# Head pairs in the softmax, norm factors moved to the evictions, and residual additions four tiles wide

## The chip, the cores and the metric

One program on one core of a Trainium2 chip (trn2). The metric is the time on the device in microseconds (us). The engines are named as the profile names them: PE (TensorE, matmuls), DVE (VectorE), ACT (ScalarE), POOL (GpSimd), SP (SyncE, which here only issues DMAs).

## What is computed

Two transformer blocks on one sequence of 256 tokens, width 2048, in float32, the second block with a memory of 256 tokens. Of the reference only what the change touches:

```python
def first_block(x, ...):
    ...
    y = merged @ w_o
    x = x + rmsnorm(y, g_post_mix)
    h = rmsnorm(x, g_pre_mlp)
    f = jnp.square(jax.nn.relu(h @ w_up)) @ w_down
    return x + rmsnorm(f, g_post_mlp)

def second_block(x, mem, ...):
    p = rmsnorm_2(x, mix_norm_w) @ w_in
    h = x + concatenate([deltanet_group(p[:DN_COLS]), rwkv7_group(p[DN_COLS:])]) @ w_out
    h = h + memory_cross_attention(rmsnorm_2(h, xa_norm_w), rmsnorm_2(mem, mem_norm_w), wq, wk, wv, wo)
    h = h + squared_relu_mlp(rmsnorm_2(h, ffn_norm_w), w1, w2)
    return rmsnorm_2(h, final_norm_w)

def rmsnorm(x, g):
    return x * lax.rsqrt(jnp.mean(x * x, axis=-1, keepdims=True) + EPS) * g

def memory_cross_attention(hn, mn, wq, wk, wv, wo):
    scores = einsum('bshd,bmhd->bhsm', hn @ wq, mn @ wk) * 128 ** -0.5
    return einsum('bhsm,bmhd->bshd', softmax(scores), mn @ wv) @ wo
```

## The kernel before

**Layout.** Activations lie transposed: a tile is 128 features (partitions) by 256 tokens, so the width 2048 is 16 tiles. `resid` holds the residual stream, `work` 64 tiles of scratch, `xa` and `xb` the inputs of the matmuls. A norm sums squares over features, that is over tiles and partitions.

**A matrix product** (class `Gemm`) is split in three. A float32 value is kept as `hi` (rounded) and `lo` (the rest), both for the weights and for the activations. SP loads a *slab*, 512 by 256 weights, into one of four ring slots (`raw`); ACT writes `hi` (L307), DVE `lo = raw - hi` (L343, the "split"); PE does 8 matmuls with `hi` on 512 columns (L428: activation `hi` and `lo`) and 8 with `lo` on 256 (L435). Two tiles of output are a *block*: 4 slabs where the depth is 2048. PE's results lie in two PSUM banks in turn (`pg`); ACT copies half of a block out (`half`, L317), DVE adds the other (the *eviction*, L348 to L397). The eviction has kinds: `store` (one DVE instruction), `add` (two), `normed` (two: sum, then times `rs`), `relu2` (four without a norm, L380 to L396; five with one).

**Order.** Each engine's queue is written out by hand, stage after stage: glu, qkv, gates, sb_out, conv_out, w_o, mem_k, mem_v, then `ff1` (four times w_up, w_down), dn, gab, rw, w_out, xa_q, xa_o, and `ff2` (four times w1, w2). A queue is strictly in order; a slab's `hi` waits until PE has used the slab four before it. What lies beside a product is hooked in: `each` is a generator that is advanced once behind every slab, `after` a function called behind every block. In every queue the next product's first slabs (`follows`) are split before the last eviction.

**Norms.** Squares come from ACT (L496, two buffers `sq`). Their sum is made by POOL into `sq_sum` (L583, for the norms in `POOLED`) and one matmul with ones (L592), or for norms 2 and 4 by 16 matmuls (`norm_pe`, L649). ACT makes `rs = exp(-0.5 * ln(...))` (L522, L523), each with a table load.

- *w_o to up0.* `norm_add_steps` (L682, L687) multiplies each tile of y by its gain and `rs` and adds it to `resid`, two tiles per slab of mem_k and mem_v, with squares and PE's sums beside. Behind mem_v `norm_split_dve` (L661, L666) and `norm_split_act` (L597) make `xa` with `rs` in it, tile by tile. POOL forms the memory's sum of squares between (L542, L547).
- *Last w_down to dn.* The same functions, with nothing beside them.
- *dn.* Behind each block DVE does a short convolution (L1082, L1084), ACT its Sigmoid (L1098), and from block 8 on squares and roots for the l2 norms (L1131, L1126, L1127, PE L1117). In rw the chunk work of the delta rule is hooked in behind slabs, and before it the gates (PE L1188).
- *Cross-attention* (`xat_pe`, `xat_act`, `xat_dve`): behind xa_q, all four heads at once: scores (L1891), transposes of the values (L1895), maximum, subtraction, Exp (L1917), sum, reciprocal, product, transposes (L1902), copy, outputs (L1909), `hi` and `lo` for xa_o.
- *xa_q and w1* already take their input without the norm factor: `xa` is `resid` times the gain (L600, L632), the root comes beside the product's first slabs (`total_later`, `root_later`), and the eviction multiplies by `rs`.

Of the kernel before, what the change touches and what calls it, by code (L numbers as in the profile page):

```python
# [132 lines left out]
def build_program(nc, a, out):  # L133
# [3 lines left out]
    with ctx:  # L137
# [396 lines left out]
        POOLED = (0, 1, 3, 5, 6, 7)  # L534
# [134 lines left out]
        def norm_add_dve(dve, n, added, tile0, gain):  # L669
            rest_of(norm_add_steps(dve, n, added, tile0, gain))  # L670

        def norm_add_steps(dve, n, added, tile0, gain, tmp=half):

            norm_rs_dve(dve, n)
            for k in range(DT + 1):
                if k and k % 2 == 0:
                    yield
                if k < DT:
                    if k >= 2:
                        dve.wait_ge(norm_res, DT * added + k - 1)  # L680
                    seq["dve"] += 1
                    nc.vector.scalar_tensor_tensor(out=tmp[:, k % 2], in0=work[:, tile0 + k, PAD:COLS],  # L682
                                                   scalar=gain(k), in1=rs[:, :], op0=ALU.mult,
                                                   op1=ALU.mult).then_inc(dve_seq, 1)
                if k:
                    dve.wait_ge(dve_seq, seq["dve"] - (1 if k < DT else 0))
                    nc.vector.tensor_tensor(resid[:, k - 1], resid[:, k - 1], tmp[:, (k - 1) % 2],  # L687
                                            ALU.add).then_inc(norm_res, 1)


# [1577 lines left out]
```

## Time and profile before

| | |
|---|---|
| median of 3 runs | 3017.79 us (3017.3 to 3023.87) |
| profiled execution | 3016.97 us, span 3014.9 us |
| PE busy | 2843.5 us, 94% of the span |
| DVE, ACT, POOL busy | 1993.4 (66%), 1439.7 (48%), 172.8 us (6%) |
| TensorE's granted clock, mean | 0.972 |
| read from HBM | 481 MB, 161 GB/s over the span |

Busy is the time in which an engine has an instruction at work. The granted clock is the share of TensorE's full clock. A wait is put down to the instruction that ended it.

### The profile page before, as it was taken

Reading aid. Unit: us, or ns where it says so; the run is one execution under the profiler, and the core shown is the slowest. Engines: PE = TensorE matmul, PEld = TensorE weight load, DVE = VectorE, ACT = ScalarE, POOL = GpSimd, SP = SyncE. Lnnn points to the kernel's source line nnn. Section 1 sums busy time; section 2 is a strip of 40 time slices with the busy share of each in tenths; the row PEclk is TensorE's granted clock in tenths of the full one; section 3 lists DMA queues with packets and bytes.
Section 4 is the critical chain, followed back from the end, with each engine's and each line's share of the span. In section 5 each row is a group of like instructions: output and inputs, shape, how many; then the busy total and the mean of one; then the engine's idle time right before and its main releaser. Section 6 shows DMA issues by size and latency. Waiting matters only on the chain.

```text
span 3014.9 us, 51495 instructions
## 1 busy us (share of the span) xinstructions
PE 2843.5 (94%) x19508; PEld 2485.8 (82%) x19508; DVE 1993.4 (66%) x2502; ACT 1439.7 (48%) x1857; POOL 172.8 (6%) x193
## 2 busy tenths in 40 slices
PE   7999999998999999999799899589979999999997
PEld 6888887877888888888688788478768888888886
DVE  6798886767646566565786666644767656566665
ACT  4545656564444444444547533634545444444443
POOL 3000000240000000001000000031112000000001
PEclk9999999999999999999899999789999999999998
DMA  5665554755666666666355444101535665656664
GB/s 186 188 195 168 175 171 137 223 169 157 190 188 189 188 187 189 188 188 188 105 181 161 128 125 128 34 4 44 163 103 181 191 189 187 189 187 190 188 188 131
DMA packets 481999, 486.66 MB, mean 161 GB/s; under 512 B 14913, under 2 KB 479809, under 8 KB 481841
## 3 DMA queue, kind: packets, MB, share of 16 engines
q1 hardware_dynamic: 480288, 478.55, 51.3%
q0 software_dynamic: 1552, 5.93, 0.6%
q8 instruction: 108, 1.77, 0.2%
q14 instruction: 51, 0.41, 0.0%
HBM read 481.28 MB, written 3.15 MB: 161 GB/s over the span
## 4 chain that ended last, share of the span: by engine, by line
PE 43%; DVE 5%; ACT 2%; issue 1%; DVEq 0%; POOLq 0%; POOL 0%; ACTq 0%
PE pg L428 24%; PE pg L435 12%; PE p L977 1%; DVE lo L343 1%; PE p L994 1%; PE p L1356 1%; PE pg L1597 0%; ACT hi L307 0%; DVE rw_xx L1048 0%; DVE half L682 0%; DVE xa L632 0%; PE p L972 0%; DVE dnc L1084 0%; PE pg L1618 0%; PE p L997 0%
## 5 line engine op out<-in xcount | busy, mean ns | idle before, releaser
L343 DVE TENSOR_TENSOR lo<-raw,hi 128x1024 fp32r<-128x1024 f32 x900 | 1091.7, 1230 | 722.5 <-ACT hi L307 718.1
L307 ACT ACTIVATE hi<-raw 128x1024 fp32r<-128x1024 f32 x900 | 942.4, 1058 | 1104.4 <-PE pg L435 1083.8
L428 PE MATMUL pg<-xa,hi 128*128 128x512 f32 x4224 | 1074.5, 396 | 16.4 <-DVE xa L666 14.2
L428 PEld LDWEIGHTS pg<-xa,hi 128*128 128x128 f32 x4224 | 764.0, 190 | 161.7 <-issue 21.8
L428 PE MATMUL pg<-xb,hi 128*128 128x512 f32 x3008 | 769.4, 398 | 31.6 <-DVE xb L487 15.5
L428 PEld LDWEIGHTS pg<-xb,hi 128*128 128x128 f32 x3008 | 549.3, 191 | 135.6 <-issue 16.6
L435 PEld LDWEIGHTS pg<-xa,lo 128*128 128x128 f32 x4224 | 577.8, 191 | 42.6 <-DVE lo L343 0.7
L435 PE MATMUL pg<-xa,lo 128*128 128x256 f32 x4224 | 590.0, 283 | 0.3 <-DVE lo L343 0.3
L435 PEld LDWEIGHTS pg<-xb,lo 128*128 128x128 f32 x3008 | 412.5, 191 | 34.5 <-DVE lo L343 4.9
L435 PE MATMUL pg<-xb,lo 128*128 128x256 f32 x3008 | 421.7, 283 | 2.8 <-DVE lo L343 2.7
L317 ACT ACTIVATE half<-pg 128x512 f32<-128x512 f32 x220 | 128.3, 583 | 91.0 <-PE pg L435 89.1
L700 DVE SCALAR_TENSOR_TENSOR work<-u,vec,work 128x256 f32<-128x256 f32 x240 | 116.2, 484 | 7.6
L360 DVE TENSOR_TENSOR half<-pg,half 128x512 f32<-128x512 f32 x96 | 65.8, 685 | 40.6 <-ACT half L317 40.1
L587 POOL COPY sq_sum<-sq 128x256 f32<-128x256 f32 x5 | 3.9, 777 | 1436.1 <-ACT sq L496 1436.1
L583 POOL TENSOR_TENSOR sq_sum<-sq_sum,sq 128x256 f32<-128x256 f32 x75 | 74.6, 995 | 178.7 <-ACT sq L496 173.9
L356 DVE TENSOR_TENSOR work<-pg,half 128x512 f32<-128x512 f32 (+1 forms) x74 | 50.5, 683 | 1.4 <-ACT half L317 1.4
L1048 DVE TENSOR_TENSOR rw_xx<-rw_xx,p 128x512 f32<-128x512 f32 x40 | 25.9, 684 | 37.3 <-PE p L997 37.1
L396 DVE TENSOR_TENSOR xb<-sq,xb 128x512 f32 (+1 forms) x64 | 44.3, 692 | 7.8 <-DVE xb L393 0.8
L362 DVE TENSOR_TENSOR resid<-resid,half 128x512 f32<-128x512 f32 (+1 forms) x56 | 41.5, 741 | 5.0 <-DVE half L360 3.9
L380 DVE TENSOR_TENSOR sq<-pg,half 128x512 f32<-128x512 f32 x64 | 43.7, 683 | 0.0
L1010 ACT ACTIVATE rw_tt<-p 128x256 f32<-128x256 f32 (+1 forms) x48 | 18.4, 383 | 48.2 <-PE p L977 39.3
L496 ACT ACTIVATE sq<-resid 128x256 f32<-128x256 f32 x80 | 31.9, 409 | 19.0 <-DVE resid L687 15.7
(401 smaller groups left out, 1709.1 us busy)
## 6 DMA issues: line engine op xcount, KB each, us to landing
raw<-w_in SPq DMA_DIRECT2D x264, 512.0 KB, 4.7
raw<-ffn_w SPq DMA_DIRECT2D x256, 512.0 KB, 4.4
raw<-w_up SPq DMA_DIRECT2D x128, 512.0 KB, 4.0
raw<-w_down SPq DMA_DIRECT2D x128, 512.0 KB, 4.3
raw<-w_o SPq DMA_DIRECT2D x32, 512.0 KB, 4.7
raw<-w_out SPq DMA_DIRECT2D x32, 512.0 KB, 3.5
raw<-w_sb_out SPq DMA_DIRECT2D x16, 512.0 KB, 4.6
raw<-w_conv_out SPq DMA_DIRECT2D x16, 512.0 KB, 4.5
```

The costliest lines, as they stand in the source:

```text
L307: nc.scalar.activation(hi[:, slot], raw[:, slot], ACT.Copy).then_inc(hi_ready, 1)
L317: nc.scalar.activation(half[:, :, :], pg[:, par, :, T:2 * T], ACT.Copy).then_inc(half_out, 1)
L343: nc.vector.tensor_tensor(lo[:, slot], raw[:, slot], hi[:, slot].bitcast(F32), ALU.subtract).then_inc(lo_ready, 1)
L356: nc.vector.tensor_tensor(place, psum, half[:, :, :], ALU.add).then_inc(evacuated, 1)
L360: nc.vector.tensor_tensor(half[:, :, :], psum, half[:, :, :], ALU.add).then_inc(summed, 1)
L362: nc.vector.tensor_tensor(place, place, half[:, :, :], ALU.add if g.kind == "add" else ALU.mult).then_inc(evacuated, 1)
L380: nc.vector.tensor_tensor(sq[:, :, :], psum, half[:, :, :], ALU.add).then_inc(summed, 1)
L396: nc.vector.tensor_tensor(rest, sq[:, :, :], place.bitcast(F32), ALU.subtract).then_inc(evacuated, 1)
L428: nc.tensor.matmul(pg[:, par, t, :], lhsT=hi[:, slot, k, c:c + P], rhs=g.x[:, kk, :], start=(j == 0 and k == 0), stop=False)
L435: ins = nc.tensor.matmul(pg[:, par, t, 0:T], lhsT=lo[:, slot, k, c:c + P], rhs=g.x[:, kk, 0:T], start=False, stop=(j == g.groups - 1 and k ...
L583: ins = nc.gpsimd.tensor_tensor(sq_sum[:, :], sq_sum[:, :], sq[:, k % 2], ALU.add)
L700: ins = nc.vector.scalar_tensor_tensor(out=acc, in0=x, scalar=v1("w_dw", 8 * j + c), in1=acc, op0=ALU.mult, op1=ALU.add)
```

## The change

Five parts:

1. `w_up` gets `norm=2`; `dn`, `gab` and `rw` change from `store` to `normed` with `norm=4`. Their input `xa` is then `resid` times the gain alone; `rs` is multiplied in at each eviction.
2. Behind w_o and behind the last w_down, ACT squares a tile of y and multiplies it by its gain in place (`y_act`), beside the product. DVE then multiplies four tiles by `rs` in one instruction (`y_scale_dve`); the addition to `resid`, four tiles wide, is DVE's for quarters 0 and 2 and GpSimd's for 1 and 3.
3. Squares of the new `resid` are taken four tiles wide into the place of y. They are added up ("folded") four tiles wide: behind w_o by GpSimd, behind w_down by DVE beside dn's first block. PE's 16 sums become one matmul. All norms are now in `POOLED`.
4. POOL does the memory's squares two tiles per step and is done with them earlier; the totals stand one slab later.
5. The cross-attention works by pairs of heads; the first pair's scores and softmax and the value transposes lie beside the second block of xa_q. The maximum goes into Exp's bias, which drops the subtraction.

```diff
-            up = Gemm(plan, f"up{p}", a["w_up"], D, p * D, D, xa, "relu2", (xb, 0, 0))
+            up = Gemm(plan, f"up{p}", a["w_up"], D, p * D, D, xa, "relu2", (xb, 0, 0), norm=2)
...
-        g_dn = Gemm(plan, "dn", w2in, D, 0, 4096, xa, "store", (work, DQ, PAD))
+        g_dn = Gemm(plan, "dn", w2in, D, 0, 4096, xa, "normed", (work, DQ, PAD), norm=4)
...
-        POOLED = (0, 1, 3, 5, 6, 7)
+        POOLED = tuple(range(8))
...
+        y4 = lambda q: work[:, YS + 4 * q:YS + 4 * q + 4, PAD:COLS]
+        resid4 = lambda q: resid[:, 4 * q:4 * q + 4]
+        def y_act(act, e, n, k, weight):
+            square_tile(act, n, k, work, PAD, YS)
+            y = work[:, YS + k, PAD:COLS]
+            nc.scalar.activation(y, y, ACT.Copy, scale=weight(k)).then_inc(y_weighted, 1)
...
+        def y_scale_dve(dve, e, q, n):
+            norm_rs_dve(dve, n)
+            dve.wait_ge(y_weighted, DT * e + 4 * q + 4)
+            nc.vector.tensor_tensor(y4(q), y4(q), rs[:, None, :].to_broadcast([P, 4, T]), ALU.mult).then_inc(y_ready, 1)
+        def y_add_dve(dve, e, q):
+            dve.wait_ge(y_ready, 4 * e + q + 1)
+            nc.vector.tensor_tensor(resid4(q), resid4(q), y4(q), ALU.add).then_inc(added_dve, 1)
+        def y_add_pool(pool, e, q):
+            pool.wait_ge(y_ready, 4 * e + q + 1)
+            nc.gpsimd.tensor_tensor(resid4(q), resid4(q), y4(q), ALU.add).then_inc(added_pool, 1)
...
+        def next_act(act, e, n, q, weight):
+            wait_added(act, e, q)
+            for k in range(4 * q, 4 * q + 4):
+                nc.scalar.activation(xa[:, k, 0:T], resid[:, k], ACT.Copy, scale=weight(k)).then_inc(norm_hi, 1)
+            nc.scalar.activation(y4(q), resid4(q), ACT.Square).then_inc(norm_sq, 4)
+        def next_dve(dve, m, q, weight):
+            for k in range(4 * q, 4 * q + 4):
+                gained_dve(dve, m, weight, k)
+        def fold(dve, e, n):
+            add = (nc.vector if e else nc.gpsimd).tensor_tensor
+            dve.wait_ge(norm_sum, POOLED.index(n))
+            steps = [(y4(0), y4(0), y4(q)) for q in range(1, 4)]
+            steps += [(work[:, YS:YS + 2, PAD:COLS], work[:, YS:YS + 2, PAD:COLS], work[:, YS + 2:YS + 4, PAD:COLS])]
...
+            add(sq_sum[:, :], work[:, YS, PAD:COLS], work[:, YS + 1, PAD:COLS], ALU.add).then_inc(norm_used, DT)
...
+            for q in (1, 3):
+                y_add_pool(pool, 0, q)
+            fold(pool, 0, 2)
...
-            norm_add_dve(dve, 3, 1, 16, lambda k: v1("g_post_mlp", k))
-            norm_rs_dve(dve, 4)
-            norm_split_dve(dve, 2, xa, resid, 0, 0, lambda k: v2("mix_norm_w_2", k), 96)
+            y_scale_dve(dve, 1, 0, 3)
+            y_add_dve(dve, 1, 0)
+            y_scale_dve(dve, 1, 1, 3)
+            next_dve(dve, 2, 0, mix_w)
+            y_scale_dve(dve, 1, 2, 3)
+            y_add_dve(dve, 1, 2)
+            y_scale_dve(dve, 1, 3, 3)
+            for q in range(1, 4):
+                next_dve(dve, 2, q, mix_w)
...
-            norm_total(pe, 3)
-            norm_pe(pe, 4)
-            gemm_pe(pe, g_dn, lambda m: l2_pe(pe, m), x_tiles=96)
+            norm_total(pe, 3)
+            def mix_total():
+                yield from skip(4)
+                norm_total(pe, 4)
+                yield
+            gemm_pe(pe, g_dn, lambda m: l2_pe(pe, m), x_tiles=96, each=step_of(mix_total()))
...
         def xat_pe(pe):
+            turn_pe(pe, 0)
             XA_.act.wait(pe, "v")
+            scores_pe(pe, 1)
+            outputs_pe(pe, 0)
+            turn_pe(pe, 1)
+            outputs_pe(pe, 1)
```

On DVE, the last block of mem_v. Before, its splits (L343) alternate with two tiles of the residual step, the multiplication (L682) and the addition (L687):

```order
L343 TENSOR_TENSOR lo<-raw,hi 128x1024 [waits hi_ready]
L682 SCALAR_TENSOR_TENSOR work<-work,vec,rs 128x256 [waits norm_res]
L687 TENSOR_TENSOR resid<-resid,work 128x256 [waits dve_seq]
L682 SCALAR_TENSOR_TENSOR work<-work,vec,rs 128x256 [waits norm_res]
L687 TENSOR_TENSOR resid<-resid,work 128x256 [waits dve_seq]
```

After, with the changed file's line numbers (L344 split, L682 `y_scale`, L618 `next_dve`, L367 and L370 eviction):

```order
L344 TENSOR_TENSOR lo<-raw,hi 128x1024 [waits hi_ready]
L682 TENSOR_TENSOR work<-work,rs 128x4x256 [waits y_weighted,norm_rs]
L344 TENSOR_TENSOR lo<-raw,hi 128x1024 [waits hi_ready]
L618 SCALAR_TENSOR_TENSOR xa<-resid,vec,xa 128x256 [waits norm_hi] x4
L344 TENSOR_TENSOR lo<-raw,hi 128x1024 [waits hi_ready]
L618 SCALAR_TENSOR_TENSOR xa<-resid,vec,xa 128x256 [waits norm_hi] x4
L344 TENSOR_TENSOR lo<-raw,hi 128x1024 [waits hi_ready]
L618 SCALAR_TENSOR_TENSOR xa<-resid,vec,xa 128x256 [waits norm_hi] x4
L367 TENSOR_TENSOR half<-pg,half 128x512 [waits half_out]
L370 TENSOR_TENSOR work<-half,work 128x2x256 [waits mem_rs,summed]
```

The fourth `y_scale` stands behind the split of slab 12, and the making of `xa` has moved from behind mem_v in between its splits 13, 14 and 15.

On PE, between the product xa_q and xa_o. Before (L1891 scores, L1895 values, L1902 transposes, L1909 outputs):

```order
L1891 MATMUL p<-work 128x256 [waits evacuated,kv_in]
L1891 MATMUL p<-work 128x256 x7
L1895 MATMUL pg<-cst,work 128x128 x8
L1902 MATMUL p<-cst,xs 128x128 [waits xat_dve]
L1902 MATMUL p<-cst,xs 128x128 x15
L1909 MATMUL p<-xp,xv 128x256 [waits xat_dve,xat_act]
L1909 MATMUL p<-xp,xv 128x256 x7
```

After, from the second slab of xa_q's last block (L1932 scores, L1938 values, L1948 transposes, L1956 outputs; L425 and L432 are the slabs):

```order
L1932 MATMUL p<-work 128x256 [waits evacuated,kv_in]
L1932 MATMUL p<-work 128x256 x3
...
L1938 MATMUL p<-cst,work 128x128 x8
...
L1948 MATMUL p<-cst,xs 128x128 [waits xat_dve]
L1948 MATMUL p<-cst,xs 128x128 x7
L1932 MATMUL p<-work 128x256 [waits evacuated,xat_act]
L1932 MATMUL p<-work 128x256 x3
L1956 MATMUL pg<-xp,xv 128x256 [waits xat_dve]
L1956 MATMUL pg<-xp,xv 128x256 x3
```

Four scores and the value transposes have moved in front of the last two slabs of xa_q; transposes and outputs come in two halves.

## Rows read from the trace of the kernel before

**Rows 1.** The page, busy us (share of the span) x instructions.

```profile
PE 2843.5 (94%) x19508; PEld 2485.8 (82%) x19508; DVE 1993.4 (66%) x2502; ACT 1439.7 (48%) x1857; POOL 172.8 (6%) x193
```

**Rows 2.** Busy time of each engine in seven stretches; columns in its head.

```profile
core 0: us, PE busy (x) PEld busy (x) DVE busy (x) ACT busy (x) POOL busy (x), PEclk, DMA share, GB/s
648.90:711.30 62.40, 56.54 (x294) 47.98 (x292) 36.50 (x55) 35.98 (x54) 7.91 (x10) 0.95 0.44 137
711.30:719.30 8.00, 0.18 (x2) 0.00 (x0) 6.34 (x13) 3.58 (x7) 0.87 (x1) 0.81 0.75 236
1435.90:1467.00 31.10, 13.72 (x39) 7.08 (x38) 19.53 (x46) 18.85 (x37) 3.60 (x4) 0.73 0.14 40
1677.80:1685.50 7.70, 0.19 (x2) 0.00 (x0) 2.36 (x6) 7.58 (x11) 0.00 (x0) 0.78 0.31 93
1685.50:1900.00 214.50, 209.09 (x2169) 184.92 (x2169) 135.53 (x200) 86.29 (x129) 0.00 (x0) 0.99 0.42 119
2218.40:2250.10 31.70, 13.74 (x58) 11.31 (x56) 14.54 (x10) 5.50 (x5) 0.00 (x0) 0.78 0.00 1
2290.00:2990.00 700.00, 700.00 (x4009) 615.93 (x4008) 442.52 (x472) 301.31 (x328) 10.49 (x12) 1.00 0.60 186
```

**Rows 3.** Waits of PE: in total, times, longest us.

```profile
PE pg L428 <- DVE xa L666: 14.2, 2, 7.9
```

**Rows 4.** Timeline of PE, w_o to up0: start, us, instructions, [idle before].

```profile
648.93 2.00 PE L428 MATMUL pg<-xb,hi 128*128 128x512 f32 x8
651.73 2.00 PE L428 MATMUL pg<-xb,hi 128*128 128x512 f32 x8
...
660.83 3.97 PE L428 MATMUL pg<-xb,hi 128*128 128x512 f32 x8
...
719.36 3.75 PE L428 MATMUL pg<-xa,hi 128*128 128x512 f32 x8 [7.88 <-DVE xa L666]
...
723.93 2.00 PE L428 MATMUL pg<-xa,hi 128*128 128x512 f32 x8
```

**Rows 5.** Three lines of code: duration ns min/median/max, first and last start.

```profile
L632 DVE SCALAR_TENSOR_TENSOR xa<-resid,vec,xa x32: 471/955/968, 2169.6 to 2287.0; 128x256 fp32r<-128x256 f32 x32
L583 POOL TENSOR_TENSOR sq_sum<-sq_sum,sq x75: 722/990/1722, 586.6 to 3001.0; 128x256 f32<-128x256 f32 x75
L1828 POOL TENSOR_TENSOR rw_br<-rw_br,cst x4: 2352/2360/2367, 1975.9 to 2067.7; 128x1024 f32<-128x1024 f32 x4
```

**Rows 6.** Timeline of DVE, the eviction of `xa_q`.

```profile
2209.69 0.68 DVE L373 TENSOR_TENSOR half<-pg,half 128x512 f32<-128x512 f32 x1
2210.41 0.69 DVE L376 TENSOR_TENSOR work<-half,rs 128x512 f32<-128x512 f32 x1
```

**Rows 7.** Timelines in dn: two of DVE, then four of ACT.

```profile
1544.47 3.50 DVE L343 TENSOR_TENSOR lo<-raw,hi 128x1024 fp32r<-128x1024 f32 x3 [1.65 <-ACT hi L307]
...
1549.43 0.68 DVE L356 TENSOR_TENSOR work<-pg,half 128x512 f32<-128x512 f32 x1
...
1542.86 0.63 ACT L1098 ACTIVATE work<-dnc 128x512 f32<-128x512 f32 x1 [5.29 <-DVE dnc L1084]
...
1554.03 0.63 ACT L1098 ACTIVATE work<-dnc 128x512 f32<-128x512 f32 x1 [5.28 <-DVE dnc L1084]
...
1607.17 0.61 ACT L1131 ACTIVATE sq<-work 128x512 f32<-128x512 f32 x1
...
1622.30 0.62 ACT L1131 ACTIVATE sq<-work 128x512 f32<-128x512 f32 x1
```

**Rows 8.** Timelines behind the last w_down: three of ACT, then PE.

```profile
1444.15 1.28 ACT L523 ACT_TABLE_LOAD   x1
1445.44 0.42 ACT L523 ACTIVATE rs<-rs 128x256 f32<-128x256 f32 x1
...
1486.51 0.63 ACT L1098 ACTIVATE work<-dnc 128x512 f32<-128x512 f32 x1 [3.51 <-DVE dnc L1084]
...
1467.01 3.72 PE L428 MATMUL pg<-xa,hi 128*128 128x512 f32 x8 [6.29 <-DVE xa L666]
```

More of the change, by code:

```diff
@@ L667, in norm_split_dve @@
                                             x[:, k - 1, 0:T].bitcast(F32), ALU.subtract).then_inc(x_ready, 1)
-        def norm_add_dve(dve, n, added, tile0, gain):
-            rest_of(norm_add_steps(dve, n, added, tile0, gain))
-        def norm_add_steps(dve, n, added, tile0, gain, tmp=half):
-            norm_rs_dve(dve, n)
[L675 to L688, printed above, removed]
+        YS = 16
@@ new lines, in turn_pe, with outputs_pe @@
+                        ins = nc.tensor.transpose(all4[:, 4 * q + 2 * kh + h % 2, m * P:(m + 1) * P],
+                                                  xs[:, 2 * h + m, kh * P:(kh + 1) * P], const("ident"))
+            XA_.pe.done(ins, f"p{q}")
+        def outputs_pe(pe, q):
+            XA_.dve.wait(pe, f"p{q}")
+            for h in heads(q):
+                for kh in range(2):
+                    ins = nc.tensor.matmul(xo_psum(q)[:, h % 2], lhsT=xv[:, h, kh], rhs=xp[:, 4 * q + 2 * kh + h % 2],
+                                           start=(kh == 0), stop=(kh == 1))
+            XA_.pe.done(ins, f"o{q}")
@@ new lines, in xat_beside_pe, with xat_pe, xat_exp @@
+        def xat_beside_pe(pe, n):
+            yield
+            yield
+            norm_total(pe, n)
+            yield
+            yield
+            yield
+            pe.wait_ge(kv_in, 16)
+            scores_pe(pe, 0)
+            yield
+            values_pe(pe)
+            yield
+        def xat_pe(pe):
+            turn_pe(pe, 0)
+            XA_.act.wait(pe, "v")
+            scores_pe(pe, 1)
+            outputs_pe(pe, 0)
+            turn_pe(pe, 1)
+            outputs_pe(pe, 1)
+        def xat_exp(act, q):
+            XA_.dve.wait(act, f"nmax{q}")
+            for i in range(4 * q, 4 * q + 4):
+                ins = nc.scalar.activation(xs[:, i], all4[:, i], ACT.Exp, scale=XA_D ** -0.5, bias=xm[:, i:i + 1])
+            XA_.act.done(ins, f"exp{q}")
@@ L2121, in post_mix @@
             def post_mix():
+                yield from skip(3)
+                y_scale_dve(dve, 0, 0, 1)
                 yield
+                y_add_dve(dve, 0, 0)
                 yield
[L2124 removed]
+                y_scale_dve(dve, 0, 1, 1)
+                yield
+                y_scale_dve(dve, 0, 2, 1)
+                yield
+                y_add_dve(dve, 0, 2)
+                yield
+                y_scale_dve(dve, 0, 3, 1)
+                yield
+                for q in range(4):
+                    next_dve(dve, 1, q, pre_mlp_w)
+                    yield
             norms = post_mix()
```

236 lines of the change are left out of this document (145 added, 91 removed).

## Prediction

> **What bounds the kernel now.** First the page's busy shares: TensorE (PE) is busy 94% of the span [rows 1]. So an edit pays only where PE waits or works for nothing. Then a table of stretches [rows 2] shows where that is. In the feed-forward of the second block PE is busy 700.0 of 700.0 us, although every eviction of `w1` there already has the form that the change gives to `w_up`. PE loses time in four places: while `mem_k` and `mem_v` run (62.4 us) and just behind them (8.0), between the last `w_down` and `dn` (31.1, of which 17.4 idle), before the gates of `rw` (7.7), and in the cross-attention (31.7, of which 18.0 idle). The waits of PE [rows 3] name one of the releasers: the `xa` tiles that DVE finishes late.
>
> What is ideal is read from PE's timeline [rows 4]: a slab of weights (8 matmuls `hi`, 8 `lo`) takes 651.73 - 648.93 = 2.79 us. Behind a pause the `hi` half alone takes 3.7 to 4.0 instead of 2.0: the 8 us pause has a granted clock of 0.81 in [rows 2], the first matmuls run at 1.2 GHz, and that costs about 1.8 us each time.
>
> **Part 1, w_o to up0.** Today slab 1 of `up0` starts at 723.93 [rows 4], 75.0 us after the first slab of `mem_k`. The change removes the pause before the totals, the 16 sums of squares by matmul between the slabs, and the wait for `xa` at 719.36. Left are 16 slabs (44.7) and two totals (about 0.9): slab 0 of `up0` could start at 694.5, slab 1 at 697.3, 26.6 us earlier.
>
> But the port stands against it. DVE and GpSimd disturb each other: the same DVE instruction of 256 columns takes 0.47 us or, in its median, 0.955; the GpSimd adds beside it take 0.72 at best and 0.99 in the median [rows 5]. The two take turns, and DVE loses 0.48, which is the 0.72 of the add less 0.24. GpSimd's additions of 1024 columns take 2.36 [rows 5]; by the same subtraction each costs a DVE instruction with two SBUF inputs 2.1 us. The lower bound is 0.48, the upper 2.36; I take 2.1, since the small add shows nearly its whole length. The Trainium skill, page "SBUF — State Buffer", section "Who interferes with whom", has this as a rule: the pair of ports goes to one of the two for a whole instruction and the other blocks fully. By that rule the price grows with the length of GpSimd's instruction, and it speaks against giving GpSimd adds four tiles wide; no row here has a long one beside such a DVE instruction.
>
> Where it bites: from the order rows DVE has, behind slab 12's split, the last `y_scale`, then split 13, four `next_dve`, split 14. Counting DVE's work from split 7 (totals behind slab 2 at 658.2, then for both roots four activations of 0.4 and three table loads of 1.28 [rows 8], one `hi` of 1.1 and the split: about 665): six splits and six wide y instructions at 1.14 [rows 7], two evictions of 1.4 [rows 6], one blocked turn of 2.1, and some 1 us of waits for ACT bring the last `y_scale` to about 684. Then GpSimd has its second residual add and five folds in a row, 4 x 2.36 + 1.3 + 0.7 = 11.5 us, and DVE gets one instruction between two of them: split 13, the four of `next_dve`, and only then split 14, done at 684 + 11.5 + 1.7 + 1.1 = 698.3. PE wants it at 648.9 + 0.9 + 14 x 2.79 + 1.84 = 690.8. A wait of 7.5 and a slow restart (1.8), and the last eviction of `mem_v` at about 704.6, put slab 0 of `up0` there and slab 1 at 707.4: **16.5 earlier**, less 0.5 for the total that PE now does inside `up0`: **-16**. Bounds: -26 (0.48 per turn, all covered by 8 us of lead) and -11 (twice the wait).
>
> **Part 2, w_up.** 32 evictions get a DVE instruction of 0.7 more, in blocks of 11.2 us whose twins leave PE without a pause [rows 2]: **0**.
>
> **Part 3, last w_down to dn.** Unchanged up to the root: `rs` is there at 1445.86 [rows 8]. Then, in us: `y_scale` 0 to 1447.1, add 0 to 1448.4, `y_scale` 1 to 1449.5; ACT's four `xa` copies from 1448.4; DVE's four `lo` parts from 1449.4, blocked once by GpSimd's add of quarter 1 (2.1), to 1453.2. Slab 0 starts there, not at 1467.01, **13.8 earlier**. It is not kept: quarter 1 comes at 1460.2 (`y_scale` 2, add 2, `y_scale` 3, four parts, one more turn of 2.1), so slab 1 waits 2.5 and restarts slowly, and slab 4 starts at 1470.3. Behind it comes the new root: total at 1473.1, Ln, table load, Exp to 1475.8, `half` 1476.3, the two-step eviction 1477.7, and the first convolution (3.4) 1481.1. That is when the first Sigmoid can run, against 1486.51 [rows 8]: **-5.4**.
>
> From there ACT and DVE set the pace, through the added 0.72 (2209.69 to 2210.41) per block [rows 6]. Their own loop today is 1.61 (Sigmoid 1542.86 to split 1544.47) + 4 x 1.14 + 4.60 (eviction 1549.43 to Sigmoid 1554.03) = 10.77 [rows 7], under PE's 11.17; with 0.72 it is 11.49. Eight such blocks take 91.9, today 89.9: **+2.0**. From block 8 to the squares before the gates the loop already bounds (15.13 between two squares [rows 7]); 7 x 0.72 less 0.9 of slack before one split: **+4.1**. So PE passes the gates at -5.4 + 2.0 + 4.1 = **+0.7**, and the 13.8 are used up. Bounds: -3 (no blocked turns, restart at full clock) and +4.
>
> In this part the root has a table load of 1.28 between Ln and Exp [rows 8]. The Trainium skill, page "ScalarE: Activation LUTs", section "Table sets: the hidden batching unit", says that one set holds both and the Exp behind a Ln needs no load. By it part 3 would come out 1.3 lower; the trace has the load, and the sum keeps it.
>
> **Part 4, rw.** 13 evictions with 0.72 more each. PE is busy 209.1 of 214.5 us here [rows 2], so most is hidden by matmuls; where DVE's chunk work is just in time it shows. Bounds 0 and 9.4; I take **+3**, nearer the lower end, as PE's idle time there is 2.5%.
>
> **Part 5, cross-attention.** In the 31.7 us window the busy times of PE, DVE and ACT, 13.7 + 14.5 + 5.5 [rows 2], add up to about the window: it is one serial chain. Half of it (15.9) remains for the second pair of heads. The first pair's scores and the value transposes are still PE time, but beside `xa_q` (2.8), and the first pair's `hi` and `lo` of the output (1.3) stand in ACT's and DVE's way: 20.0, plus 0.7 for smaller instructions. **-11**, bounds -13 and -8.
>
> **Sum.** -16 + 0 + 0.7 + 3 - 11 = -23.3. The profiled execution took 3016.97 (span 3014.9), 0.8 under the median of 3017.79; so 2993.7 against the first and **2994.5** against the median.
>
> **Rivals.** (A) *GpSimd's long adds cost DVE no more than short ones*, 0.48 a turn: part 1 gives 26, part 3 about -2.5: -26 - 2.5 + 3 - 11 = -36.5, 2981. For it: no row of a long block; against it: 0.48 is two thirds of 0.72. The page on SBUF, by its rule of the whole instruction, speaks against it too. (B) *Every longer eviction of dn, gab and rw is on the path*: 30 x 0.72 = 21.6 instead of the 9.1 above: -10.8, 3007. For it: at dn's blocks the loop has 0.4 us of slack; against it: PE at 97% in rw. (C) *The cross-attention does not overlap*, since ACT's `half` of the second `xa_q` block stands behind four Exps and the value copy: part 5 gives nothing, -12.3, 3005.5. Against it: `half` can't be due before PE's last slab, and the Exps end some 3 us earlier. (D) *Slower*: in dn, gab and rw PE now waits a little in each block instead of running through, and if the clock falls to 1.2 GHz each time, 30 blocks pay 1.8: +54 - 23 = +31, 3049. It decides from 13 such blocks on (13 x 1.8 = 23). Against it: between 1685.5 and 1900, with its many short waits, the granted clock is 0.99 [rows 2]; it is low (0.81, 0.73, 0.78, 0.78) only in the four stretches in which PE stood idle.
>
> **How the numbers follow.** A measurement of this kernel can tell 0.2%, 6 us, from no change. Chances: the forecast 0.62, A 0.18, B 0.12, C 0.04, D 0.04. The forecast's own bounds (-11 and -26 in part 1, the others in part) give 2984 to 3003; with A and half of B, the range is 2978 to 3007. Faster by over 6 us: the forecast, A, B and C but for their upper ends, 0.92; the same 0.04; slower 0.04.
>
> **What would show it.** Right: DVE's instructions of `next_dve` at 2 us and more while GpSimd folds, and a PE wait for a `lo` split some 42 us after `mem_k` starts; `dn`'s first slab about 17 us behind the last `w_down`, but the gates of `rw` reached no earlier, counted from there, than before; PE's window of the cross-attention at about 21; the second feed-forward unchanged. Wrong: if PE runs through `mem_v` and `up0` without a pause (A), if rw grows by more than 6 (B), or if PE's clock lies under 0.95 in dn or rw (D).

## The result, and the profile after

The changed kernel takes 2993.58 us in the median of 4 runs (2991.91 to 2994.07), the kernel before 3017.55 (3014.51 to 3023.87, also 4): a ratio of 0.992, with a 95% interval from 0.9907 to 0.9932. It is faster by 24 us, and the forecast was 2994.5. The profiled execution has a span of 2990.7 us, 24.2 less than before. One execution of the kernel before beside the experiments took 9362 us and is left out of every median named here.

The page of the kernel after, busy us (share of the span) and instructions, answers to [rows 1]:

```profile
PE 2824.6 (94%) x19448; PEld 2473.1 (83%) x19448; DVE 2025.7 (68%) x2492; ACT 1446.3 (48%) x1871; POOL 195.4 (7%) x202
```

PE's share of the span is again 94%. A table of busy times by stretch, kernel after, with its columns in the head. The first stretch is `mem_k` and `mem_v` up to `up0`; then come the one from the last `w_down` to `dn`, `rw` from the gates to the end of its matmuls, the end of xa_q's last slab to xa_o, and a part of the second feed-forward:

```profile
core 0: us, PE busy (x) PEld busy (x) DVE busy (x) ACT busy (x) POOL busy (x), PEclk, DMA share, GB/s
648.10:702.80 54.70, 48.10 (x262) 41.78 (x261) 42.49 (x39) 37.95 (x57) 19.23 (x11) 0.94 0.42 134
1418.60:1436.20 17.60, 1.25 (x3) 0.56 (x3) 9.95 (x11) 11.90 (x24) 6.13 (x5) 0.59 0.19 60
1667.90:1885.70 217.80, 211.30 (x2174) 186.71 (x2174) 144.63 (x212) 86.36 (x129) 0.00 (x0) 0.99 0.38 117
2206.10:2225.90 19.80, 10.23 (x43) 7.92 (x41) 9.15 (x12) 4.20 (x8) 0.00 (x0) 0.83 0.00 0
2265.00:2965.00 700.00, 700.00 (x4011) 616.01 (x4010) 443.02 (x473) 301.73 (x328) 9.46 (x12) 1.00 0.59 186
```

Against [rows 2], the gap in front of `dn` has gone from 31.1 us to 17.6, and what stands between xa_q and xa_o from 31.7 to 19.8 (2.5 us of that only moved to a place ahead of xa_q's end, so the gain is 9.5); in the second feed-forward PE is busy all the time, as before.

For the rest of this text both traces are divided at the same instructions, so that a difference belongs to the stretch in which it arises (us):

| stretch (PE, where no other engine is named) | before | after | after - before | forecast |
|---|---|---|---|---|
| start to the first slab of `mem_k` | 648.93 | 648.12 | -0.81 | 0 |
| on to slab 1 of `up0` | 75.00 | 57.59 | **-17.41** | -16.5 |
| on to the last matmul of `w_down` | 712.45 | 712.89 | +0.44 | +0.5 |
| on to slab 0 of `dn` | 30.63 | 17.57 | **-13.06** | -13.8 |
| on to the first Sigmoid (ACT) | 19.50 | 26.62 | +7.12 | +8.4 |
| on to the ninth Sigmoid, with the squares behind it | 89.86 | 91.90 | +2.04 | +2.0 |
| on to the gates | 109.18 | 113.27 | +4.09 | +4.1 |
| `rw`, to the end of its matmuls | 215.33 | 217.78 | +2.45 | +3 |
| preparation of the recurrence of rwkv7 | 30.76 | 29.23 | -1.53 | 0 |
| the recurrence | 186.00 | 187.87 | +1.87 | 0 |
| on to slab 0 of `xa_q` | 77.73 | 77.72 | 0.0 | 0 |
| slab 0 of `xa_q` to slab 0 of `xa_o` | 54.79 | 45.31 | **-9.48** | -11 |
| the rest | 764.7 | 764.8 | +0.1 | 0 |

In this table "the recurrence" runs from the end of PE's wait of some 13 us for `rw_d` to the first slab of the second half of `w_out`, and "preparation" is what lies between `rw` and it.

**The wait ahead of up0.** PE's timeline of the kernel after (start, us, instructions, idle before and what ended it). `mem_k` begins at 648.12:

```profile
648.12 2.00 PE L425 MATMUL pg<-xb,hi 128*128 128x512 f32 x8
...
688.10 2.00 PE L425 MATMUL pg<-xb,hi 128*128 128x512 f32 x8
696.70 2.08 PE L432 MATMUL pg<-xb,lo 128*128 128x256 f32 x8 [6.59 <-DVE lo L344]
698.57 3.31 PE L425 MATMUL pg<-xb,hi 128*128 128x512 f32 x8
...
705.71 2.00 PE L425 MATMUL pg<-xa,hi 128*128 128x512 f32 x8
```

One pause of 6.59 us is left, where the forecast had 7.5, ended by DVE's split 14. What DVE and GpSimd did then, DVE's timeline and behind it GpSimd's (POOL), kernel after:

```profile
684.27 2.62 DVE L618 SCALAR_TENSOR_TENSOR xa<-resid,vec,xa 128x256 fp32r<-128x256 f32 x1
686.81 2.63 DVE L618 SCALAR_TENSOR_TENSOR xa<-resid,vec,xa 128x256 fp32r<-128x256 f32 x1
689.37 2.59 DVE L618 SCALAR_TENSOR_TENSOR xa<-resid,vec,xa 128x256 fp32r<-128x256 f32 x1
691.88 2.56 DVE L618 SCALAR_TENSOR_TENSOR xa<-resid,vec,xa 128x256 fp32r<-128x256 f32 x1
694.36 2.28 DVE L344 TENSOR_TENSOR lo<-raw,hi 128x1024 fp32r<-128x1024 f32 x1
...
683.13 3.48 POOL L690 TENSOR_TENSOR resid<-resid,work 128x1024 f32<-128x1024 f32 x1 [8.17 <-DVE work L682]
686.57 8.99 POOL L717 TENSOR_TENSOR work<-work 128x1024 f32<-128x1024 f32 x4
```

Each of the four `next_dve` instructions lasts 2.6 us, though alone it takes 0.47 [rows 5], and the split behind them 2.28 instead of 1.2. They run one for one beside the residual addition and the three folds of 1024 columns, the split beside the fold of 512. So a GpSimd addition of 2.36 us costs DVE 2.62 - 0.47 = 2.15; forecast was 2.1, by subtracting the same 0.24 as for the small add. Rival A, 0.48 each, is out. The Trainium skill, page "SBUF — State Buffer", section "Who interferes with whom", has the rule that one of the two engines gets the shared pair of ports for a whole instruction and the other blocks fully. These rows agree with it: 2.15 us of 2.36.

**dn.** PE's first slabs of `dn`, then ACT's squares of the l2 norms, kernel after:

```profile
1436.17 3.75 PE L425 MATMUL pg<-xa,hi 128*128 128x512 f32 x8 [9.62 <-DVE xa L618]
1439.72 1.91 PE L432 MATMUL pg<-xa,lo 128*128 128x256 f32 x8
1443.40 2.10 PE L425 MATMUL pg<-xa,hi 128*128 128x512 f32 x8 [1.77 <-DVE xa L618]
...
1446.29 2.00 PE L425 MATMUL pg<-xa,hi 128*128 128x512 f32 x8
...
1571.09 0.61 ACT L1168 ACTIVATE sq<-work 128x512 f32<-128x512 f32 x1
...
1586.95 0.61 ACT L1168 ACTIVATE sq<-work 128x512 f32<-128x512 f32 x1
...
1602.80 0.61 ACT L1168 ACTIVATE sq<-work 128x512 f32<-128x512 f32 x1
```

Slab 1 waits 1.77 us for its `xa`, behind a slow slab 0 (3.75 instead of 2.00 for the `hi` half). The squares are 15.86 apart, where [rows 7] have 15.13: 0.73 more, the length of the second eviction instruction. In the blocks ahead the period is (1554.69 - 1462.79) / 8 = 11.49, the forecast number.

**Cross-attention.** PE's timeline of the second pair, kernel after, and behind it the first 11 of 16 transposes, and the outputs, of the kernel before:

```profile
2210.34 1.89 PE L1956 MATMUL pg<-xp,xv 128*128 128x256 f32 x8
2217.43 1.97 PE L1948 MATMUL p<-cst,xs 128*128 128x128 f32 x8 [5.21 <-DVE xs L2017]
2220.72 3.47 PE L1956 MATMUL pg<-xp,xv 128*128 128x256 f32 x8 [1.32 <-DVE xp L2022]
2225.87 2.10 PE L425 MATMUL pg<-xb,hi 128*128 128x512 f32 x8 [1.69 <-ACT hi L308]
```

```profile
2237.67 2.61 PE L1902 MATMUL p<-cst,xs 128*128 128x128 f32 x11 [10.66 <-DVE xs L1931]
2243.82 3.69 PE L1909 MATMUL p<-xp,xv 128*128 128x256 f32 x16 [2.47 <-DVE xp L1934]
```

The last line ahead of `xa_o` takes 3.47 us for the 8 matmuls that took 1.89 at 2210.34. TensorE had been idle for 5.21 and 1.32 of the 8.5 us since 2212.2, and nearly double the time puts these at the lower clock of 1.2 GHz for the most part. In the kernel before the 16 transposes behind the long pause were the slow ones (2.61 us for the first 11, 3.68 for all; in the kernel after 8 take 1.04 at full clock and 1.97 behind the pause), and the 16 outputs behind them ran at full clock.

### The profile page after: what moved, and what is told of

Its sections match the earlier page's. It is cut to its first block, busy times and chain, and to the rows that moved or that the text cites. A ratio compares the mean times of both kernels' runs of the same rounds, so it can differ in the third digit from the quotient of the medians.

```text
span 2990.7 us, 51348 instructions
## 1 busy us (share of the span) xinstructions
PE 2824.6 (94%) x19448; PEld 2473.1 (83%) x19448; DVE 2025.7 (68%) x2492; ACT 1446.3 (48%) x1871; POOL 195.4 (7%) x202
## 4 chain that ended last, share of the span: by engine, by line
PE 81%; DVE 11%; ACT 4%; issue 2%; POOL 1%; DMA 0%; ACTq 0%; DVEq 0%; POOLq 0%; SPq 0%
PE pg L425 49%; PE pg L432 25%; DVE lo L344 4%; ACT hi L308 1%; DVE dnc L1121 1%; PE p L1014 1%; PE p L1031 1%; DVE xa L618 1%; PE p L1393 1%; DVE work L377 1%; DVE half L374 0%; POOL sq_sum L476 0%; PE pg L1634 0%; ACT L1163 0%; DVE work L737 0%
## 5 line engine op out<-in xcount | busy, mean ns | idle before, releaser
L344 DVE TENSOR_TENSOR lo<-raw,hi 128x1024 fp32r<-128x1024 f32 x900 | 1089.9, 1232 | 680.3 <-ACT hi L308 675.7
L425 PE MATMUL pg<-xa,hi 128*128 128x512 f32 x4224 | 1074.9, 397 | 15.0 <-DVE xa L618 13.5
L425 PEld LDWEIGHTS pg<-xa,hi 128*128 128x128 f32 x4224 | 764.0, 190 | 162.6 <-issue 22.2
L425 PE MATMUL pg<-xb,hi 128*128 128x512 f32 x3008 | 765.5, 397 | 32.2 <-DVE xb L484 16.2
L425 PEld LDWEIGHTS pg<-xb,hi 128*128 128x128 f32 x3008 | 547.4, 191 | 134.9 <-issue 17.6
L432 PEld LDWEIGHTS pg<-xa,lo 128*128 128x128 f32 x4224 | 578.5, 191 | 42.7 <-DVE lo L344 0.7
L432 PE MATMUL pg<-xa,lo 128*128 128x256 f32 x4224 | 590.8, 283 | 0.3 <-DVE lo L344 0.3
L432 PEld LDWEIGHTS pg<-xb,lo 128*128 128x128 f32 x3008 | 413.9, 192 | 41.3 <-DVE lo L344 11.9
L432 PE MATMUL pg<-xb,lo 128*128 128x256 f32 x3008 | 423.8, 284 | 9.4 <-DVE lo L344 9.3
L618 DVE SCALAR_TENSOR_TENSOR xa<-resid,vec,xa 128x256 fp32r<-128x256 f32 x64 | 50.2, 839 | 0.0
L384 DVE SCALAR_TENSOR_TENSOR sq<-sq,rs 128x512 f32<-128x512 f32 x64 | 44.3, 692 | 2.2
L388 DVE TENSOR_TENSOR sq<-sq 128x512 f32<-128x512 f32 x64 | 44.3, 692 | 2.2
```

The lines of the kernel that those rows point to most:

```text
L344: nc.vector.tensor_tensor(lo[:, slot], raw[:, slot], hi[:, slot].bitcast(F32), ALU.subtract).then_inc(lo_ready, 1)
L425: nc.tensor.matmul(pg[:, par, t, :], lhsT=hi[:, slot, k, c:c + P], rhs=g.x[:, kk, :], start=(j == 0 and k == 0), stop=False)
L432: ins = nc.tensor.matmul(pg[:, par, t, 0:T], lhsT=lo[:, slot, k, c:c + P], rhs=g.x[:, kk, 0:T], start=False, stop=(j == g.groups - 1 and k ...
L618: nc.vector.scalar_tensor_tensor(out=xa[:, k, T:2 * T], in0=resid[:, k], scalar=gain(k), in1=xa[:, k, 0:T].bitcast(F32), op0=ALU.mult, op1 ...
```

## The experiments

Each kernel was timed beside the kernel before on the same chip, and not all on one chip; the kernel before took 3016.1 to 3017.8 us in the median there, 3017.55 beside the change. So a comparison "against the change", which takes the median 2993.58, carries some 1.5 us of doubt from this alone. Two control runs come first, since all the others are read with them.

**Control.** The changed kernel again, and with one exchange that lies behind all but the last quarter of the program.

```diff
             xat_max(dve, 1)
-            xat_lo(dve, 0)
             xat_div(dve, 1)
+            xat_lo(dve, 0)
```

> The changed kernel once more, as a control. A stretch that no edit touches, the recurrence of rwkv7 (from PE's wait of some 13 us for rw_d to the first slab of w_out's second half), took 186.0 us before, 187.9 with the change, 182.9, 191.1 and 187.7 in three of the experiments, with a granted clock of 0.90 where it was short and 0.85 where it was long. Theory (the clock in this stretch of small matmuls depends on how the kernel comes into it, and is the same each time the same kernel runs): 187.9 within 1 us, and every other stretch within 0.3 us. Rival (it is chance from execution to execution): another value between 183 and 191.

> The changed kernel with one exchange in DVE's queue in the cross-attention: the lo of the first pair's output behind the second pair's sum, reciprocal and product. Theory (the lo and its wait for ACT's hi stand 1.1 us in the second pair's chain, and fit beside PE's transposes): the stretch from xa_q's first slab to xa_o's falls from 45.3 to 44.2 us. Rival (the second pair's chain is set by PE or ACT there): 45.3. Everything ahead of the cross-attention as in the changed kernel, the recurrence stretch too.

Measured: 2994.61 us (2992.74 to 2996.72) and 2992.27 (2988.93 to 2993.27). Of the stretches of the table ahead of `xa_q`, all but the recurrence agree with the change's within 0.2 us in both. Behind it, the stretch from `xa_o` to the first slab of `w1` took 28.0 us in the first control, against the 0.3 us of leeway expected, and 26.5 in the second and in the change. The recurrence took 187.87, 189.04 and 185.57 us in the three profiles, though up to its end the three kernels are the same code. So the theory of the first run falls: the length is chance from one execution to the next, by 3.5 us in these three. The rows of this stretch in two of the kernels below, no wide work on GpSimd (first) and the kernel before with another order in dn (second), whose instructions in it are the same:

```profile
1903.40:2094.90 191.50, 146.54 (x3377) 130.99 (x3377) 97.39 (x135) 65.59 (x117) 40.06 (x46) 0.88 0.06 19
```

```profile
1925.30:2102.90 177.60, 136.22 (x3377) 122.24 (x3377) 96.64 (x135) 65.31 (x117) 40.06 (x46) 0.93 0.06 20
```

DVE, ACT and GpSimd are busy for the same time within 1 us; PE is busy 10 us longer where its granted clock was 0.88 instead of 0.93. In all profiles of this study the stretch took between 177.6 and 191.5 us. Whether all of these 14 us are chance, or the edits ahead of the stretch have a share in them, the runs do not show. The Trainium skill, page "TensorE: Matmul & The Clock Gate", section "Part 1: The HAM clock gate", says that the number of slow matmuls at a kernel's start varies from run to run. No run here looks at a kernel's start; the three profiles of the same code show a like variation in the middle of a kernel, 185.57 to 189.04 us. The exchange itself gave what its theory said: `xa_q` to `xa_o` fell from 45.31 (45.63 in the first control) to 44.29. From here on a verdict rests on the edited stretch, and the total only confirms it.

**The fold on DVE.** The squares of norm 2 are folded by DVE in pieces, each behind a split:

```diff
-            add = (nc.vector if e else nc.gpsimd).tensor_tensor
+            add = nc.vector.tensor_tensor
...
                 add(o, x, y, ALU.add).then_inc(folded, 1)
+                if i < 3:
+                    yield
...
                 for q in range(4):
                     next_dve(dve, 1, q, pre_mlp_w)
                     yield
+                yield from fold(dve, 0, 2)
```

> The changed kernel, but the five additions that fold the squares of the second norm run on DVE, one behind each of the next splits, instead of on GpSimd; its total follows after slab 4 of up0. Theory (the port: a four-tile addition on GpSimd holds DVE for its whole length): DVE's split 14 is done at about 689, PE's wait of 6.6 us for it goes, slab 1 of up0 starts 48 to 50 us behind mem_k's first slab instead of 57.6, and the time falls by 7 to 9 us although DVE has 5 us more of work. Rival (DVE is late because it has too much work of its own there): the 5 us more come on top, the wait stays or grows, and the time rises by 0 to 5 us.

Measured: 2984.05 us (2983.24 to 2990.76), 9.5 under the change; slab 1 of `up0` 49.67 us behind `mem_k`'s first slab, 7.9 less than with the change. DVE's timeline there:

```profile
685.19 3.81 DVE L618 SCALAR_TENSOR_TENSOR xa<-resid,vec,xa 128x256 fp32r<-128x256 f32 x4
688.93 1.21 DVE L344 TENSOR_TENSOR lo<-raw,hi 128x1024 fp32r<-128x1024 f32 x1
690.06 1.66 DVE L618 SCALAR_TENSOR_TENSOR xa<-resid,vec,xa 128x256 fp32r<-128x256 f32 x4
```

Only the first of the four is still blocked, by the residual addition (3.81 for the four against 1.66 for the next). DVE got 5 us more of work and was done with split 14 sooner, at 690.1 instead of 696.6. That rules out the rival and shows GpSimd's additions as the cause of the wait. Beyond the 7.9 us the profile has chance in it: the recurrence took 182.94 us, 4.9 less than with the change, while the first slabs of `dn` and the stretch from `xa_o` to `w1` took 1.5 and 2.8 more.

**Narrow folds.** The same additions on GpSimd, tile by tile:

```diff
+            y1 = lambda k: work[:, YS + k, PAD:COLS]
+            if not e:
+                for i in range(14):
+                    k = i % 4
...
+                    add(y1(k), y1(k), y1(4 + i if i < 12 else k + 2), ALU.add).then_inc(folded, 1)
```

> The changed kernel, but GpSimd folds tile by tile: 14 additions and a last one, of 256 columns, instead of three of 1024, one of 512 and one of 256. Theory (DVE loses the length of each addition less 0.24 us, whatever its width): an instruction of next_dve takes 0.95 instead of 2.6, the wait for split 14 falls from 6.6 to about 1.3 us, but the 15 short turns cost DVE 15 x 0.48 = 7.2 us where the wide ones cost 7.9, spread over the next splits; slab 0 of up0 starts within 1.5 us of where it does now, and the time changes by -1.5 to 0 us. Rival (it is the width that hurts): PE runs through, and the time falls by 5 to 8 us.

Measured: 2995.83 us (2994.26 to 2997.7), 2.2 over the change, where -1.5 to 0 was expected. DVE's timeline:

```profile
684.75 2.62 DVE L618 SCALAR_TENSOR_TENSOR xa<-resid,vec,xa 128x256 fp32r<-128x256 f32 x1
687.29 0.96 DVE L618 SCALAR_TENSOR_TENSOR xa<-resid,vec,xa 128x256 fp32r<-128x256 f32 x1
...
689.95 1.76 DVE L344 TENSOR_TENSOR lo<-raw,hi 128x1024 fp32r<-128x1024 f32 x1
691.63 3.59 DVE L618 SCALAR_TENSOR_TENSOR xa<-resid,vec,xa 128x256 fp32r<-128x256 f32 x4
...
700.28 0.68 DVE L367 TENSOR_TENSOR half<-pg,half 128x512 f32<-128x512 f32 x1
```

Here three instructions of four take 0.96 and the waits of PE are 1.16 at slab 14, 2.13 at slab 15 and 3.60 at `up0`. Slab 1 of `up0` stands 57.65 us behind `mem_k`, with the change 57.59. So the stretch did what the theory says, and it is the sum of the blocked turns that counts, not the width of one. The total missed its range; in the profile, whose span is 3.8 us longer than the change's, 3.2 of that is the recurrence (191.07 against 187.87).

**No wide work on GpSimd.** The fold as above, and all residual additions on DVE (shown for the second norm pair, behind the last w_down):

```diff
-            for q in (1, 3):
-                y_add_pool(pool, 1, q)
...
             next_dve(dve, 2, 0, mix_w)
+            y_add_dve(dve, 1, 1)
             y_scale_dve(dve, 1, 2, 3)
+            next_dve(dve, 2, 1, mix_w)
             y_add_dve(dve, 1, 2)
```

> The fold on DVE as in the first experiment, and all eight residual additions four tiles wide on DVE too, so GpSimd does none of the wide work. Theory (a wide addition costs DVE 2.1 us when GpSimd does it and 1.14 when DVE does it itself): PE's last wait of 1.05 us before up0 goes, slab 1 of up0 starts 48 to 49 us behind mem_k's first slab; behind the last w_down dn's first slab comes 1.5 to 2.5 us earlier (15 to 16 us instead of 17.6) and the first Sigmoid 2 to 4 us earlier, and in all the time falls by 11 to 13 us against the change. Rival (GpSimd does real work beside DVE, which DVE now has on top): up0 and dn no earlier than with the fold alone, or later.

Measured: 2981.25 us (2977.9 to 2984.86), 12.3 under the change. `up0`'s slab 1 comes at 48.82, `dn`'s slab 0 at 15.48 behind the last `w_down` (17.57 with the change). Both hold. The first Sigmoid gained 1.7 instead of 2 to 4: PE now waits 1.86 us for the total of norm 4, whose fold comes later on a DVE with more to do. The edited stretches give 10.5 us up to the gates; that the total shows 12.3 is within its own spread, for the four runs lie in two pairs, 2978 and 2984 to 2985.

**The factor in the eviction.** The multiplication by `rs` is left out in `dn`, `gab` and `rw`, so these outputs lack it:

```diff
-        g_dn = Gemm(plan, "dn", w2in, D, 0, 4096, xa, "normed", (work, DQ, PAD), norm=4)
+        g_dn = Gemm(plan, "dn", w2in, D, 0, 4096, xa, "store", (work, DQ, PAD))
```

> The changed kernel with the multiplication by rs left out in the evictions of dn, gab and rw, so these outputs lack the norm's factor; all else stays. Theory (in dn the loop of DVE and ACT is 11.49 us with the multiplication and 10.77 without, so PE's 11.17 bounds; from block 8 on it is on the loop; in rw mostly hidden): first Sigmoid 2 to 3 us earlier, 2.5 us in the eight blocks behind it, 4 to 5 us from there to the gates, about 3 us in rw: the time falls by 10 to 13 us. Rival B (each of the 30 evictions is on the path): 21.6 us. Rival (all of it is hidden): under 3 us.

Measured: 2983.32 us (2982.3 to 2983.48), 10.3 under the change, but in the profile 4.7 of that are the recurrence, so the total falls into its range of 10 to 13 by chance. From `dn`'s slab 0 to the gates 226.5 us instead of 231.8, 5.3 less; in `rw` 1.65 less. The first Sigmoid came not 2 to 3 us earlier but 2.0 later; the eight blocks behind it gave 4.8 instead of 2.5, the way from there to the gates 2.5 instead of 4 to 5. TensorE's clock came back late in this execution. PE's timeline, `dn`'s first slabs:

```profile
1437.04 3.50 PE L425 MATMUL pg<-xa,hi 128*128 128x512 f32 x8 [9.62 <-DVE xa L618]
1440.38 1.11 PE L432 MATMUL pg<-xa,lo 128*128 128x256 f32 x8
1444.26 3.75 PE L425 MATMUL pg<-xa,hi 128*128 128x512 f32 x8 [2.77 <-DVE xa L618]
1447.81 1.91 PE L432 MATMUL pg<-xa,lo 128*128 128x256 f32 x8
1449.52 2.40 PE L425 MATMUL pg<-xa,hi 128*128 128x512 f32 x8
```

Slab 2 starts 12.48 us behind slab 0, in the change 10.12 (1446.29 - 1436.17). With these 2.4 the factor costs 5.3 to 7.7 in dn, where the forecast had 2.0 + 4.1.

In rw too the clock has a share. The first slab behind the gates, `hi` and `lo` half, in the kernel before and then in the kernel after:

```profile
1686.04 3.47 PE L428 MATMUL pg<-xa,hi 128*128 128x512 f32 x8
1689.34 1.11 PE L435 MATMUL pg<-xa,lo 128*128 128x256 f32 x8
```

```profile
1668.45 3.78 PE L425 MATMUL pg<-xa,hi 128*128 128x512 f32 x8
1672.03 1.91 PE L432 MATMUL pg<-xa,lo 128*128 128x256 f32 x8
```

The `lo` half of the second slab starts 6.79 us behind the gates before and 8.07 after; 7.62 without the factor, and 8.29 in the kernel before with another order in dn (below), whose evictions have no factor. The rest of `rw` behind that instruction takes 209.7 us in all nine kernels with the factor and 208.5 in all three without. So the factor costs 1.2 us in rw, and 6.5 to 8.9 in all; forecast were 2.0 + 4.1 + 3 = 9.1. The 21.6 of rival B are out.

**Roots first, then a late Sigmoid.** Two edits of ACT's queue in dn. The first:

```diff
             def conv_l2(m):
-                dn_conv_act(act, m)
                 l2_act(act, m)
+                dn_conv_act(act, m)
```

> The changed kernel with two calls exchanged in ACT's queue in dn: behind each block the root of the l2 norm and its squares come before the Sigmoid instead of behind it. Theory (from block 8 on ACT's Ln and Exp with two table loads, 3.9 us, stand between the Sigmoid and the next hi, on a loop of 15.86 us, while ACT idles some 4 us before the Sigmoid for DVE's convolution): the three periods of 15.86 become about 12 and the four of 11.98 about 11.2: the gates come 11 to 15 us earlier, and the time falls by as much. Rival (ACT's busy time bounds these blocks, or PE's sums of squares come too late then): no change within 2 us.

The second on top:

```diff
                 l2_act(act, m)
-                dn_conv_act(act, m)
+                late.append(m)
+
+            def beside_dn():
+                if late:
+                    dn_conv_act(act, late.pop())
+                next(root4, None)
+            late, root4 = [], mix_root()
-            gemm_act(act, g_dn, conv_l2, follows=g_gab, each=step_of(mix_root()))
+            gemm_act(act, g_dn, conv_l2, follows=g_gab, each=beside_dn)
+            dn_conv_act(act, late.pop())
```

> The changed kernel with the roots before the Sigmoid, and the Sigmoid one slab later in ACT's queue, behind the next hi. Theory (DVE waits 1.65 us in each block of dn for a hi that stands behind the Sigmoid, so the loop of 11.49 falls below PE's 11.17 once this is gone): the eight periods of 11.49 become 11.17, which brings 2.5 us up to block 8, and from there PE bounds at 11.17 and, with the sum of squares between, 12.0: the gates come 2 to 4 us earlier than with the roots first alone, 15 to 17 us earlier than with the change. Rival (the loop is bound by DVE's own work or by the ring of four slabs): periods stay at 11.49, nothing beyond the roots.

Measured: 2980.27 us (2979.66 to 2981.2) and 2975.7 (2974.17 to 2978.34), 13.3 and 17.9 under the change. From the first Sigmoid to the gates: 205.17 us with the change, 191.81 and 188.50 with the edits. ACT's timeline with both edits, the first two Sigmoids of dn and then its last blocks:

```profile
1463.26 0.64 ACT L1135 ACTIVATE work<-dnc 128x512 f32<-128x512 f32 x1 [2.64 <-DVE dnc L1121]
...
1473.61 0.63 ACT L1135 ACTIVATE work<-dnc 128x512 f32<-128x512 f32 x1 [4.50 <-DVE dnc L1121]
...
1607.03 0.62 ACT L1168 ACTIVATE sq<-work 128x512 f32<-128x512 f32 x1
1607.55 1.04 ACT L308 ACTIVATE hi<-raw 128x1024 fp32r<-128x1024 f32 x1
1608.61 1.28 ACT L1140 ACT_TABLE_LOAD   x1
1609.91 0.63 ACT L1140 ACTIVATE dnc<-work 128x512 f32<-128x512 f32 x1
1610.44 2.00 ACT L308 ACTIVATE hi<-raw 128x1024 fp32r<-128x1024 f32 x2
...
1619.07 0.62 ACT L1168 ACTIVATE sq<-work 128x512 f32<-128x512 f32 x1
```

The period at the end is 1619.07 - 1607.03 = 12.04, PE's own: four slabs and a sum of squares. The first Sigmoids are 10.35 apart: with the loop loosened they catch up with a PE that has run ahead, and only then take its 11.17. So the eight periods gave 5.2 us and not the expected 2.5. Behind slab 1, the profile shows no further wait of PE until the gates. So what bounded dn was the loop over ACT and DVE and not the work of either.

**The same edits without the change.** The kernel before, with both edits of ACT's queue:

> The kernel before, with only the roots before the Sigmoid and the Sigmoid one slab later. Theory (before, dn's late start was followed by a PE that mostly kept its own pace up to block 8, and then lost to ACT's chain; with the chain gone PE bounds all of dn, with and without the factor in the eviction): from dn's first slab to the gates 211 to 213 us instead of 218.5, the time 3009 to 3012. Then the change on top of this edit is worth 34 to 36 us, not 24, since the 13.8 us of the earlier first slab are kept. Rival (the order of ACT's queue helps only the changed kernel, whose loop it relieves): within 2 us of before.

Measured: 3009.26 us (3003.79 to 3015.59, 10 runs), a ratio of 0.9977 (0.9967 to 0.9987). `dn`'s slab 0 to the gates takes 211.93 us instead of 218.54. So the change on top of these edits is worth 3009.3 - 2975.7 = 33.6 us (34.6 if each is first taken against the kernel before on its own chip), against 24 alone; by stretches, from the last `w_down` to the gates 242.6 and 232.7, the change gains 9.9 where alone it gained nothing (249.2 and 249.4).

**All together.**

> All of it together: no wide work on GpSimd, roots before the Sigmoid and the Sigmoid one slab later, lo of the first pair later. Theory (the gains lie in different stretches and add up: 8.8 us ahead of up0, 2.1 ahead of dn, 16.7 between dn's first slab and the gates, 1.0 in the cross-attention): 28 to 29 us less than the change, 2963 to 2967 us, 52 less than before. Rival (in dn the earlier start is not kept, or the total of the fourth norm, which waits 1.9 us for its fold, takes back what the start gains): 2967 to 2970.

Measured: 2963.4 us (2962.71 to 2968.27), a ratio of 0.9831 (0.9818 to 0.9845) to the kernel before. The edited stretches give -8.8 ahead of `up0`, -2.1 ahead of `dn`, -16.3 up to the gates and -0.9 in the cross-attention, -28.0 together, of the 30.2 by the medians. This version beats both kernels, the changed one by 30 us.

## Why the prediction was right, step by step

- **Part 1**, forecast -16.5 up to slab 1 of `up0`: -17.4. Split 14 was forecast done at 698.3 and was done at 696.6, PE's wait 7.5 and was 6.6. The step that carried it, a long GpSimd instruction costs DVE its length less 0.24 us, was an extension from an add of 0.72 to one of 2.36, and held (2.15 for 2.1). The fold on DVE showed these instructions as the cause of the wait.
- **Part 2**, forecast 0: the stretch grew by 0.44, which is the total that part 1 had put at 0.5 there.
- **Part 3**, forecast +0.7 up to the gates: the four terms measured -13.06 + 7.12 + 2.04 + 4.09 = +0.2. The gain ahead of `dn` was real and was used up: 7.1 us because the first Sigmoid comes later behind slab 0, the rest by longer periods. Both are the loop's doing, for it is too slow to make up a late first Sigmoid. The two kernels with the late Sigmoid show this: without the loop 9.9 us of the gain stay. The experiment had expected all 13.8 to stay; slab 1 of `dn`, which waits for its `xa` and restarts slowly, takes part of it (7.2 us behind slab 0 instead of 4.5).
- **Part 4**, forecast +3: +2.45 in `rw`. That the two are close is luck. The factor, which the term was for, cost 1.2; the other 1.3 are a slower return of the clock behind the gates, which the forecast did not have and which the kernel before shows as well once its order in dn is changed.
- **Part 5**, forecast -11, measured -9.48. This term was mis-sized by 1.5 us. The chain is as described, but the forecast put down half of what followed xa_q before. Half of the outputs would be 3.69 / 2 = 1.85, and they took 3.47, 1.6 more. The forecast left out that with half as many transposes ahead of them the outputs run before the clock is back. That this is the cause is read from the rows; no run here takes the pause away.
- **The sum** was -23.3, the profiles show -24.2. That agreement is closer than its terms deserve. Part 1 gave 1 us more than forecast and part 5 gave 1.5 less. In stretches that the change does not touch, -0.8, -1.5 and +1.9 us nearly cancel; the -1.5 are 16 matmuls of the preparation that took 6.73 us before and 5.20 after. And two executions of one kernel differ by more than the 0.9 between forecast and result.
- **Rivals.** A fell with 2.15 per turn; B with the run without the factor; C with 45.3 instead of 54.8; D with a granted clock of 0.99 in `rw` and 0.96 in dn (1436.2 to 1668).

## What to carry to other kernels

When DVE's work is given to GpSimd beside DVE instructions with two SBUF inputs, it costs DVE nearly the summed length of GpSimd's instructions, whatever their width; here DVE lost 2.15 us to an addition that it would have done itself in 1.14. An earlier start is kept only if the stages behind it have slack: look for the period of the loop behind, before counting the gain, and for what in a strictly ordered queue stands between one engine's result and the other's next piece. Read experiments of a few us by stretches between the same instructions, for a total carries the chance of stretches that no edit touches.

## What the runs showed of the hardware

- A DVE instruction with two SBUF inputs and a GpSimd addition took turns, DVE held up for the addition's length less 0.2 us or so: DVE's 0.47 us became 0.96 beside additions of 256 columns and 2.62 beside 1024, and GpSimd's addition of 256 columns took 0.92 beside such a short DVE instruction and 1.71 beside a split of 1024 columns. The eviction's first instruction, with one input in PSUM, kept its 0.68 us at 700.28 of the kernel with narrow folds while GpSimd added.
- The return of TensorE's clock behind a pause is not the same in two executions: in `dn`, slab 2 began 10.07 to 10.12 us behind slab 0 in six profiles, and 11.67 and 12.48 in two, behind the same wait of 9.6 us ahead of slab 0.
- The partly idle recurrence, the same code throughout, took 177.6 to 191.5 us over twelve kernels, with granted clocks of 0.85 to 0.93, and 185.6 to 189.0 in three kernels that are the same up to its end.
- On ACT each of the 17 Exps of a root has a table load of 1.28 us between it and its Ln, in every kernel here. The sum of part 3 was right to keep it. In the last blocks of dn, with the queue in the better order, three loads a block are hidden behind PE.
